# First block's norm and its q and k products placed among the steps of the context's second routing

## The reference

```python
# first block
h = rmsnorm(x, g_mix) * (1 + scale1) + shift1
proj = h @ w_in
q, k, v, u, vs, ga, gb = jnp.split(proj, splits, axis=-1)     # q, k, v, u, vs: 512 columns each
...
# second block, for each 128 tokens of x or of the context
s_top, i_top = lax.top_k(s, 16)                                # 8 heads, 2 halves, 128 keys
cand = s_top[:, :, 0, :, None] + s_top[:, :, 1, None, :]
best, pos = lax.top_k(cand, 16)                                # 8 x 16 experts of each token
u = jnp.take(u_tab, eid, axis=0)
act = gelu(einsum('chkd,cd->chk', u, hc)) * softmax(best)
v = jnp.take(v_tab, eid, axis=0)
return einsum('chk,chkd->cd', act, v)
```

## Time and profile before

| | us |
|---|---|
| median of 3 runs | 3821.81 |
| lowest and highest | 3816.61, 3829.53 |
| the profiled execution | 3827.01 |
| its span | 3825.3 |
| PE, DVE, ACT, POOL busy | 2651.7, 1810.1, 502.2, 1481.5 |
| mean of what all DMA moved over the span | 274 GB/s |

### The profile page before, as it was taken

The page is one execution under the profiler, slowest core; times in us unless marked ns, Lnnn a source line. Parts: engine busy times, 40 slices in busy tenths (PEclk is TensorE's granted clock), DMA queues, the critical chain, the costliest instruction groups (busy, mean ns, idle before and its releaser), DMA issues.

```text
span 3825.3 us, 35082 instructions
## 1 busy us (share of the span) xinstructions
PE 2651.7 (69%) x11672; PEld 1361.5 (36%) x11672; DVE 1810.1 (47%) x4395; ACT 502.2 (13%) x1117; POOL 1481.5 (39%) x1577
## 2 busy tenths in 40 slices
PE   4899747989999888885565555457788455555555
PEld 3367513456666534674121000004377400000000
DVE  1521586443333577217774444443711795444444
ACT  1220101320100124001020000002210100000000
POOL 0000045443444443200555666661000066666665
PEclk8899857899999988997667666668699766666666
DMA  7668469878999985631789999993023089999998
GB/s 255 229 224 317 178 233 333 319 285 324 348 352 352 335 289 199 218 139 46 285 324 338 356 359 359 363 358 139 33 94 121 29 325 361 361 360 355 360 361 331
DMA packets 325906, 1047.09 MB, mean 274 GB/s; under 512 B 27424, under 2 KB 38752, under 8 KB 325728
## 3 DMA queue, kind: packets, MB, share of 16 engines
q0 software_dynamic: 240192, 880.90, 62.1%
q1 hardware_dynamic: 85536, 163.95, 12.3%
HBM read 1043.70 MB, written 1.05 MB: 273 GB/s over the span
## 4 chain that ended last, share of the span: by engine, by line
PE 38%; DVE 22%; issue 13%; another core or an unknown queue 12%; DMA 5%; PEld 4%; ACT 2%; PEldq 2%; SPq 1%; ACTq 0%; DVEq 0%; POOL 0%; POOLq 0%
PE ps L378 18%; DVE UV L953 8%; PE ps L401 5%; PE ps L416 5%; PEld ps L378 4%; DMA W<-in_w_in 3%; PE ps L370 3%; DVE arena L1191 2%; PEldq L365 2%; PE ps L503 1%; DVE arena L1290 1%; DVE arena L1296 1%; DVE arena L1287 1%; PE ps L680 1%
## 5 line engine op out<-in xcount | busy, mean ns | idle before, releaser
L953 DVE SCALAR_TENSOR_TENSOR UV<-ps,UV 128x1024 f32<-128x1024 f32 x768 | 913.3, 1222 | 1045.3 <-remote 561.0
L1905 POOL DMA_INDIRECT UV<-in_u_tab,idxT x768 | 725.1, 944 | 1530.0 <-DVEq L1364 766.0
L401 PE MATMUL ps<-hs,selb 96*128 96x512 bf16 x1536 | 586.0, 494 | 700.4 <-DVE UV L953 375.8
L1915 POOL DMA_INDIRECT UV<-in_v_tab,idxT x768 | 723.8, 943 | 418.3 <-issue 206.9
L378 PE MATMUL ps<-H,W 128*128 128x256 f32 (+2 forms) x3296 | 684.0, 370 | 73.7 <-DMA W<-in_w_in 45.8
L378 PEld LDWEIGHTS ps<-H,W 128*128 128x128 f32 (+1 forms) x3296 | 587.4, 199 | 184.6 <-issue 58.3
L401 PEld LDWEIGHTS ps<-hs,selb 96*128 96x128 bf16 x1536 | 122.7, 108 | 1279.9 <-DVE UV L953 713.2
L416 PE MATMUL ps<-UV,acts 128*32 128x512 f32 x3072 | 538.4, 781 | 36.6 <-issue 24.8
L378 PE MATMUL ps<-arena,W 128*128 128x256 f32 (+1 forms) x1632 | 370.9, 385 | 21.6 <-issue 11.1
L378 PEld LDWEIGHTS ps<-arena,W 128*128 128x128 f32 (+1 forms) x1632 | 304.9, 190 | 107.4 <-issue 62.6
L1502 ACT ACTIVATE arena<-ps 128x512 f32<-128x512 f32 (+7 forms) x310 | 167.5, 550 | 999.5 <-PE ps L378 783.3
(11 more groups left out here) (154 smaller groups left out, 1771.9 us busy)
## 6 DMA issues: line engine op xcount, KB each, us to landing
W<-in_w_in SPq DMA_DIRECT2D x30, 2048.0 KB
UV<-in_w_mod POOLq DMA_DIRECT2D x24, 2048.0 KB, 14.1
W<-in_w_ff SPq DMA_DIRECT2D x16, 2048.0 KB
UV<-in_w_ada POOLq DMA_DIRECT2D x12, 2048.0 KB, 11.9
W<-in_w_out SPq DMA_DIRECT2D x8, 2048.0 KB
W<-in_w_query SPq DMA_DIRECT2D x6, 2048.0 KB
UV<-in_u_tab,idxT POOLq DMA_INDIRECT x768
UV<-in_v_tab,idxT POOLq DMA_INDIRECT x768
```

Of the source, the lines that this page charges most:

```text
L401: last = mm(ps[:, HB + 2 * (tok % 2) + hf, :], one, hs[:, n % 2, t // GROUP, hf * 512:(hf + 1) * 512], start=True, stop=True)
L953: dve.scalar_tensor_tensor(out=Us[:, j, :], in0=ps[:, b:b + 2, :].rearrange("p a b -> p (a b)"), scalar=1.0, in1=Us[:, j, :], op0=MUL, op1 ...
L1905: pool.indirect_dma_start(Us[:, j, :], None, A["u_tab"], off).then_inc(sem(f"u_arrived{j}"), 16)
L1915: pool.indirect_dma_start(Vs[:, j, :], None, A["v_tab"], off).then_inc(sem(f"v_arrived{j}"), 16)
```

## The change

The norm of the first block and its products `in1` 0 (q) and `in1` 1 (k) leave `first_block` and are done inside the routing of tile 1: the norm behind step `top 0` and its beat, `in1` 0 behind `top 2`, `in1` 1 behind `pairs 2`. It is written so on PE, DVE and ACT alike; `first_block` goes on with `in1` 2. The squares of the norm are kept in H itself instead of in the arena, so that ACT needs no wait for `idx_ready` before them; that wait now stands at the head of ACT's `first_block`. The lists of SP and POOL are not changed.

```diff
-        SQ = {("f", "n1"): view(0, DT, SEQ), ("f", "n2"): view(3072, DT, SEQ), ("f", "n3"): view(4096, DT, SEQ)}
+        SQ = {("f", "n1"): H[:, :, :], ("f", "n2"): view(3072, DT, SEQ), ("f", "n3"): view(4096, DT, SEQ)}
...
-            def routes(n):
+            def routes(n, beside={}):
 
                 for i in range(2, len(STEPS) - 1):
                     beat((STEPS[i], n), 8.4)
+                    for piece in beside.get(STEPS[i], ()):
+                        piece()
...
+            def first_products(j):
+
+                w = weights(("in1", j))
+                for d in range(2):
+                    duo(("in1", j, d), w, [(2 * d + e) * P for e in range(2)], H, DT, first=(j + d == 0))
+                    beat(("in1", j, d), 7.0)
+                done_with_weights()
+
+            BESIDE = {"top 0": [lambda: norm("f", "n1")], "top 2": [lambda: first_products(0)], "pairs 2": [lambda: first_products(1)]}
 
             def first_block():
 
-                norm("f", "n1")
-                for j in range(5):
+                for j in range(2, 5):
...
-            route_second("c0")
+            route_second("c0", BESIDE)
             first_block()
```

On DVE:

```diff
                 for step in STEPS[at:-1]:
                     route(n, step)
                     beat(step, n)
+                    for piece in beside.get(step, ()):
+                        piece()
                 route(n, "experts")
...
+            def first_norm():
 
                 prepare("f", "n1")
                 sq_base[0] += DT
                 norm("f", "n1")
-                for j in range(5):
-                    for t in range(2):
-                        beat("in1", j, t)
+
+            def first_products(j):
+
+                for t in range(2):
+                    beat("in1", j, t)
```

On ACT:

```diff
+            def first_norm():
 
                 act.wait_ge(sem("x_loaded"), 16)
-                act.wait_ge(sem("idx_ready"), 2)
                 for u in range(4):
                     square("f", "n1", u)
                 norm("f", "n1")
...
+            def first_block():
+
+                act.wait_ge(sem("idx_ready"), 2)
+                first_products(range(2, 5))
```

More of the change, by code:

```diff
@@ L788, in route_first, with route_second @@
                 routes(n)
-            def route_second(tag):
+            def route_second(tag, beside={}):
                 n = TILE_OF[tag] + 1
@@ L794, in route_second @@
                 scores(n)
-                routes(n)
+                routes(n, beside)
+            def first_products(j):
[5 more added lines that the diff above has]
+            BESIDE = {"top 0": [lambda: norm("f", "n1")], "top 2": [lambda: first_products(0)], "pairs 2": [lambda: first_products(1)]}
             def first_block():
-                norm("f", "n1")
-                for j in range(5):
+                for j in range(2, 5):
+                    if j == 3:
+                        first_products(j)
+                        continue
                     w = weights(("in1", j))
-                    if j in (2, 4):
-                        for t in range(2):
[L804 to L810, removed]
+                    for t in range(2):
+                        o = bank(("in1", j, t))
+                        full(acc_mm(o, [H[:, k, t * P:(t + 1) * P] for k in range(DT)], [w[:, k, :] for k in range(DT)]), ("in1", j, t))
+                        beat(("in1", j, t), 7.0)
                     done_with_weights()
@@ L1370, in hidden, with routes @@
                 beat("ht", n)
-            def routes(n, at):
+            def routes(n, at, beside={}):
                 for step in STEPS[at:-1]:
@@ L1396, in route_second @@
                 beat("sc", n)
-                routes(n, 2)
-            def first_block():
+                routes(n, 2, beside)
+            def first_norm():
                 prepare("f", "n1")
@@ L1403, in first_block @@
                 norm("f", "n1")
-                for j in range(5):
-                    for t in range(2):
-                        beat("in1", j, t)
+            def first_products(j):
+                for t in range(2):
+                    beat("in1", j, t)
+            BESIDE = {"top 0": [first_norm], "top 2": [lambda: first_products(0)], "pairs 2": [lambda: first_products(1)]}
+            def first_block():
+                for j in range(2, 5):
+                    first_products(j)
                 dve.wait_ge(sem("vs_squares"), 1)
@@ L1806, in first_block, with first_products @@
                 norm("f", "n1")
-                for j in range(5):
+            BESIDE = {"top 0": [first_norm], "top 2": [lambda: first_products([0])], "pairs 2": [lambda: first_products([1])]}
+            def first_products(these):
+                for j in these:
                     for t in range(2):
```

## The result

The changed kernel takes 3841.97 us (median of 11 runs, 3832.30 to 3849.52), the kernel before 3822.57 us beside it (11 runs, 3806.96 to 3834.87). The ratio is 1.0047, 95% interval 1.0034 to 1.0059: slower by 18 us (13 to 23). The forecast was 3832 us, +10.2. On two other chips, where the kernel before takes 3665 us, the same pair gave 1.0027 (1.0015 to 1.0039) and 1.0028 (1.0017 to 1.0039), +10 us each time.

What follows compares the result with a forecast made beforehand. DVE bounds the routing of tile 1, PE the first products; their chain moves the end one for one. Routing +48.6, wait at `in1` 2 +18.6, removed stretch -57.0: +10.2 on 3821.8, so 3832 us, range 3817 to 3846.

Steps and rivals of the forecast that it cites:

- The frame: From the routing's last write to `in1` 2: 57.0 us vanish, 48.6 of longer routing and 18.6 of waiting replace them.
- Everything later is as before: Behind `in1` 2: both orders have done 23 visits there, so every later stage keeps its length.
- Visits and norm: In the routing of tile 1, on DVE: seven more visits add 16.5 us, the norm 6.7 us.
- Standing of DVE: In the routing, DVE waits for PE's spread at the four halves of `in1` 0 and `in1` 1: 25.4 us together.
- The rival with the clock up: Products in the routing: PE gets busier, clock up and transfer short; +2 us, 3824 us; chance 0.10.
- the row of 9.99 us: First half of `in1` 0 in the old profile, at 634.92 us: 9.99 us at the low clock, against 7.17 high.
- Wait for the chunk: At `in1` 2, behind the routing's last write: 6.8 us of issue, 9 transfer, 2.8 slow start, 18.6 in all.
- the second of the two rules weighed: Chunk of `in1` 2: DMA engines alternate between queues; with gathers queued it gets about half rate, sum about +15.
- The faster one: In the routing: DVE does not stand at the beats, halves lie wholly beside steps; -15 us, 3807 us; chance 0.08.
- The small one: Products and chunk of `in1` 2: clock up and transfer short; +2 us, 3824 us, shows as no change; chance 0.10.
- The clearly slower one: Weight ring: chunk of `in1` 2 lands 13.8 us behind issue, halves run longer; about +20, 3842 us; chance 0.12.
- A result within 0.3%: Whole kernel: a difference within 0.3%, 11.5 us, about what a measurement can tell from no change; chance 0.52.

Runs made afterwards that it cites:

- e4: The changed kernel with the four beats of `in1` 0 and `in1` 1 counting 0 us instead of 7; ratio to the kernel before 0.9994.
- e9: The changed kernel with each half of `in1` 0 and `in1` 1 summed over 4 of 8 blocks, so half-length products; ratio to the kernel before 0.9998.
- e1: The changed kernel with SP's wait for `idx_ready` 2 and the ten constant loads moved behind the chunk of `in1` 3; ratio to the kernel before 0.9982.
- e5: The changed kernel with the edits of e1, e3 and e4 together, run twice; ratio to the kernel before 0.9926 and 0.9913.
- e7: The kernel before with 60 small memsets on DVE, each waited for, ahead of the first block's norm; ratio to the kernel before 1.0073.
- before_again: The kernel before, unchanged, run once more on one of the other chips for its trace and scatter; ratio 1.0001.
- e3: The changed kernel with each half of `in1` 0 and `in1` 1 behind its own step (`top 2`, `top 3`, `pairs 2`, `pairs 3`); ratio to the kernel before 1.0022.
- after_third: The changed kernel as it is, measured for the third time, on the chip of before_again; ratio to the kernel before 1.0028.
- after_again: The changed kernel as it is, measured again on another chip than the first pair's; ratio to the kernel before 1.0027.

## Why the prediction was right, and where it was off

**The frame held up to `in1` 2.** Its second half starts 12.3 us later in the first pair, 9.7 and 10.8 us on the other chips, for +10.2 forecast (that sum held the slow first half, so this is the mark to compare). Its two costs beside visits and norm are each shown by a run that takes them away: the standing by e4 and e9, the wait for the chunk by e1, both by e5.

**"Everything later is as before": not borne out.** The first gather of tile 2 moved by 13.8 us in the first pair, and e7 shows that a long delay goes on whole to it. But I had named a later stage that takes up or gives back more than 3 us as a sign of being wrong, and there are several: in the first pair's traces the delay is 12.3 us at `in1` 2, 17.7 at the first feed-forward chunk, 13.8 at that gather and 8.2 at the end; e7 loses 2 to 6 us behind the gather. The total is right on the other chips all the same.

**Visits and norm: right.** 23 visits by the end of the routing, the sum of squares hidden by `top 0` with 4.9 us to spare. The routing is 49.0 us longer for 48.6 forecast in the first pair, 44.5 and 42.8 us on the other chips.

**Standing of DVE: right in kind and in its places, the terms off.** I put 6.0, 6.5, 5.7 and 7.2 us, with both first halves at 9.99 us. The first halves took 7.17 and 7.99 us; the granted clock by window (start:end, length, busy us of PE, PEld, DVE, ACT, POOL, PEclk, DMA share, GB/s) in the changed kernel:

```profile
568.00:571.00 3.00, 3.00 (x20) 0.47 (x12) 2.97 (x15) 0.20 (x1) 2.38 (x3) 0.82 0.75 247
571.00:574.00 3.00, 3.00 (x16) 2.39 (x13) 2.90 (x19) 0.00 (x0) 2.09 (x3) 1.00 0.99 341
...
604.00:607.00 3.00, 3.00 (x14) 1.72 (x7) 2.86 (x13) 0.00 (x0) 1.98 (x3) 0.56 0.80 262
```

The first half of `in1` 0 began at 2.4 GHz, behind two visits done back to back; that of `in1` 1 behind a single one, at the low level for about the 1.6 us that its 0.82 us of extra length amount to (an estimate from 7.99 - 7.17). The rival with the clock up was right in this term. The Trainium skill ("TensorE: Matmul & The Clock Gate", Part 1) ties the clock to how busy TensorE has lately been. The trace of the changed kernel agrees, 7.17 and 7.99 us right behind visits; I had weighed that rule and gone by the row of 9.99 us. I had also read that row as "right behind" matmuls and visits, and it shows 3.10 us of idleness ahead, which these two halves do not have. Idleness alone does not settle it, though: before_again has 3.02 us of it in that place and took 7.51 us.

At 7.17 us my terms give 19.8 us; the other chips show 21.1 and 19.1. In the first pair the total was 24.4 us all the same, since two of the four waits (6.37 and 8.70 us) are longer than product and spread explain. So 25.4 was near by an offset, not by insight. What lengthened those two stays open. In the first, ACT's copy of the product is late too (583.49 us, behind a product that the record ends at 578.5), and PE's outputs there are drawn out, from 580.45 to 584.35 us instead of 1.06, as in e3. So PE was late, at full clock (1.00 from 578 to 584 us); no row shows why. Of the four waits forecast at 5 to 8 us and released by the spread, the first pair has one that is both, 5.94 us.

**Wait for the chunk: right in cause, too short.** Forecast 6.8 us of issue, 9 us of transfer, 2.8 us of slow start, 18.6 in all; measured 6.5 + 11.9 + 1.95 = 20.3 us (12.3 us of transfer in after_third). The term that was mis-sized is the transfer: I took a value between the idle row and the one beside gathers, because gathers should be over once their slots are full. They were not at first. Two windows of the changed kernel, and below them the view of the DMA queues (packets, MB, share of the 16 engines' time) from 675 to 678 us and from 678 to 681 us; q0 carries the gathers, q1 SP's loads:

```profile
672.00:675.00 3.00, 0.00 (x0) 0.00 (x0) 0.00 (x0) 0.00 (x0) 0.00 (x0) 0.50 1.03 406
675.00:678.00 3.00, 0.00 (x0) 0.00 (x0) 0.00 (x0) 0.00 (x0) 0.00 (x0) 0.50 1.07 340
...
q0 software_dynamic: 208, 0.72, 65.4%
q1 hardware_dynamic: 575, 0.30, 42.0%
...
q1 hardware_dynamic: 555, 1.05, 104.7%
```

PE and DVE stand still and the DMA engines run at full share. GpSimd issued its last gather at 669.33 us, and rows for it were moved until 678 us; up to there the gathers' queue took about two thirds of the engines' time, and behind it SP's queue had all of it. So the chunk, issued at 672.73, shared for 5.3 us and ran alone for the last 6.7: both rows that I chose between are in it, one behind the other. Of the constants' 1 MB, issued ahead of it in the same queue, 0.45 MB had been moved by 672.7 us. This is the sharing that the second of the two rules weighed speaks of; the forecast did not follow it. The nearest row was that with gathers, 13.8 us.

**From +12 to +18 in the first pair: open.** There the ratio stands for 18 us (13 to 23), 12.3 are in place at `in1` 2. On the other chips total and shift at `in1` 2 agree. In the two traces of the first pair the delay wanders (17.7 us is read at the issue of the first feed-forward chunk, 964.22 against 946.54 us) by as much as is to be explained. That products which wait for weights beside gathers add something at 355 GB/s and not at 402 would fit, but no run here shows it.

**The rivals.** The faster one (DVE never stands) fell: it stands, and e9 ties it to the products' length. It nearly comes true in e5, where the places are changed. The small one had the clock right and the transfer wrong. The clearly slower one named a chunk that lands late beside gathers, which is what happened, though without the slow halves that it added; its 3842 us lies at the median of the first pair, for partly other reasons, and that is luck. A result within 0.3% had the larger chance in my forecast (0.52); the first pair misses it with its whole interval, and the ratios of the other chips meet it, with intervals that reach 0.4%.

## What to carry to other kernels

Where engines meet in a fixed order, work placed "beside" a step hides only if no meeting point stands behind it before the other engine has something of its own to do: here a product, then a beat, then another product left the second with no cover at all, and four waits of 3 to 9 us ate the gain. When work is moved ahead of a wait in another queue, read that queue's list to the end: here SP's wait for the routing's end had cost nothing while the products stood behind the same point, and cost 18 us once they did not. When such a move comes out as a small loss, it may be two small faults on a sound idea: mending both gave 27 to 32 us against the kernel before. And a sum that comes out right is not yet a sum of right terms: on the other chips the same +10 us was made of 44 and 54 us instead of 49 and 57.

## What the runs showed of the hardware

Chips differ by 4% to 5% on the same kernel (3822.57 and 3842 against 3665 us), and the difference goes with the rate of the transfers, 355 against 402 GB/s from 2000 to 2400 us: of the 161 us between the spans of before and before_again only 8.6 lie ahead of the first gather of tile 2 (1823.93 against 1815.37 us). Why the rates differ is not shown. The chunk behind the routing gained nothing by it: 11.9 us in after, 12.2 and 12.3 us in after_again and after_third. On the slower chips DVE's waits at its dots without a named releaser are longer in the changed routing (7.3 us in the changed kernel, 19.2 us in e3, 0.2 us in before); on the other chips there are none in either trace of the changed kernel.

A load that SP issues while gathers are still queued shares the DMA engines with them until they run out (65.4% to 42.0% of the engines' time from 675 to 678 us in after) and has them alone from then on (104.7%). Gathers ran on for some 8 us behind the issue of the last one by GpSimd (669.33 us, in after).
